# Stick-breaking attention: key evacuation, split weights and sample sums reordered, half of the sample key products moved to GpSimd

## The chip, the cores and the metric

One core of one Trainium2 chip runs the whole program: two layers of a small decoder for a prompt of 512 tokens and 8 sample tokens. The metric is the device time of one execution in microseconds (us). Only the attention of layer 0 is touched.

## The reference, cut to what matters

Each of the 8 samples has one query and 512 past positions in 4 cached pages of 128. Per head, the score is the dot product of the query with every cached key; a sigmoid of it, times the product of the complements of all later positions, weighs the cached values. The prompt's 512 tokens do the same among themselves.

```python
z = jnp.einsum('bqhd,bkhd->bhqk', q, k).astype(jnp.float32) * scale + bias
log_not = jnp.where(mask, jax.nn.log_sigmoid(-z), 0.0)
after = lax.cumsum(log_not, axis=3, reverse=True) - log_not
a = jnp.where(mask, jnp.exp(jax.nn.log_sigmoid(z) + after), 0.0)
return jnp.einsum('bhqk,bkhd->bqhd', a.astype(v.dtype), v)
```

## The kernel before

The channels are split into 8 head pairs (`hp`, 0 to 7). Attention is a loop over them written out by hand, one list of steps per engine, joined by semaphores. Each list is executed strictly in its order, so a step that waits holds everything behind it on its engine.

In pass `hp` the prompt's attention for head pair `hp` runs: scores (TensorE, `scores`), two sigmoids for each of five score units (ScalarE, `sigmoids`), a running product and the weights (VectorE, `later_product`, a scan, and `weights`), transposes of the weights (TensorE and ScalarE, `turned`), outputs (`output_a`, `output_b`). Between them TensorE computes the k and v of head pair `hp + 1` in eight pieces, `chunk(hp, 0..7)`: pieces 0 to 3 make k, pieces 4 to 7 make v. Weights are kept as a high and a low part: ScalarE's `split_hi` (L227) and VectorE's `split_lo` (L231, `w_lo<-w_raw,w_hi`). VectorE's `next_v(hp)` makes the low part that `chunk(hp, 4)` waits for, `next_k(hp)` that of the next pass. `k_evac` (L293, `s_up<-ps,rms`) takes k out of PSUM; ScalarE squares it (`k_squares`, L1074), TensorE sums over heads (`k_sums`, L800), ScalarE takes the root (`k_factor`, L1081 and L1083), VectorE's `ready` (L1266) normalizes, and TensorE transposes it in `k_turned` (L825).

The same loop carries sample `hp` and, ahead of it, the scores of sample `hp + 1`. SyncE spreads the sample's query over 128 partitions into `q_bc` (it lies in the tile `p_tok`), and loads four key pages into `kc`, 128x1024 each. `page_scores(b, g)` multiplies page g by the query in place (L1330) and reduces over each head (L1335). In pass 0 VectorE does all four pages of sample 0 as well as those of sample 1. `page_sums` (L1347 to L1353) prepares later-position sums, TensorE's `sample_sums` (L956 and L957) adds them up, `page_weights` (L1358) subtracts them; the next `k_turned` waits for that, since they share a PSUM bank. `sample_exp` (ScalarE, L1180) makes the weights of the sample, `sample_values` and `sample_output` (TensorE) apply them. Keys of the next sample are loaded page by page by `next_keys`, each page after the reduction of the old one. GpSimd does nothing in this loop except one memset at its start (L1438).

The order of VectorE's list behind the last weights of a pass is:

```python
weights(hp, 4); next_v(hp)
# pass 0 only: page_scores(0, 0..3), page_bias(0)
k_evac(hp + 1); next_k(hp)
page_scores(hp + 1, 0); ready(hp + 1)
page_scores(hp + 1, 1); page_sums(hp)
page_scores(hp + 1, 2); sample_lo(hp - 2)
page_weights(hp); pair_lo(hp)
page_scores(hp + 1, 3); page_bias(hp + 1)
```

TensorE's list in the same place is `turned` 0, 1, 2, `k_sums(hp + 1)`, `turned` 3, `chunk` 4, `turned` 4, `chunk` 5, `sample_output(hp - 2)`, `output_a`, `chunk` 6, `output_b`, `sample_sums(hp)`, `k_turned(hp + 1)`, `chunk` 7.

Of the kernel before, what the change touches and what calls it, by code (L numbers as in the profile page):

```python
# [22 lines left out]
NS = 8  # L23
# [25 lines left out]
def build(nc, io):  # L49
# [4 lines left out]
    with ctx:  # L54
# [3 lines left out]
        def sem(name):  # L58
            return ctx.enter_context(nc.semaphore(name))
# [604 lines left out]
        k_out = sem("k_out")  # L664
        v_out = sem("v_out")
        kq_ok = sem("kq_ok")
        z_mm = sem("z_mm")
        sm_ok = sem("sm_ok")
        sg_ok = sem("sg_ok")
# [31 lines left out]
            return ps[:, 2 + r // 2, r % 2, :]  # L701

        cs_ps = ps[:, 0, 1, HALF:HALF + PG * NH]

        def os_at(b):
            return bank(min(b + 2, NP - 1), OS)[:, 0:KD]
# [10 lines left out]
        def attn_sp(sp):  # L717
            n0 = M["slab"]

            def kv(hp, c):  # L720
                load_slab(sp, n0 + NP + 2 * hp + c, c, qkv_src(1 + c, hp), KD)

            def page_of(cache, dst, done, b, g):

                page = sp.value_load(pages[0:1, b * PG + g:b * PG + g + 1], min_val=0, max_val=cache.shape[1] - 1)
                rows = cache[0].rearrange("n p h d -> n p (h d)")[ds(page, 1), :, :]
                sp.dma_start(dst[:, g, :], rows.rearrange("a p f -> p (a f)")).then_inc(done[g], 16)

            def k_page(b, g):
                page_of(io["cache_k"], kc, k_cache_in, b, g)  # L730

            def v_page(b, g):
                page_of(io["cache_v"], vc, v_cache_in, b, g)

            def q_spread(b):
                sp.dma_start(q_bc, q_rows[b:b + 1, :].broadcast_to([P, D])).then_inc(q_bc_in, 16)

            for m in range(NP):
                load_slab(sp, n0 + m, m % 2, qkv_src(0, m), KD)
            sp.wait_ge(first_in[3], 16)  # L740
            sp.wait_ge(slab_used, n0)
            for g in range(PG):
                k_page(0, g)
            for g in range(PG):
                v_page(0, g)
            for hp in range(2):
                for c in range(2):
                    kv(hp, c)
            for c in range(2):
                sp.wait_ge(qt_ok, c + 1)  # L750
                sp.dma_start(q_rows[:, c * TP:(c + 1) * TP], q_row[c]).then_inc(q_rows_in, 16)
            sp.wait_ge(q_rows_in, 32)
            q_spread(0)

            def next_keys(b):
                sp.wait_ge(kq_ok, PG * b)
                q_spread(b)
                for g in range(PG):
                    sp.wait_ge(zs_ok, 5 * (b - 1) + g + 1)
                    k_page(b, g)  # L760

            for hp in range(NP):
                if hp + 2 < NP:
                    kv(hp + 2, 0)
                elif hp + 2 == NP:
                    load_slab(sp, n0 + 3 * NP, 0, slab_src(io["attn_w_o"][0], 0), KD)
                if hp >= 2:
                    sp.wait_ge(sv_mm, hp - 1)
                    for g in range(PG):
                        v_page(hp - 1, g)  # L770
                if hp + 2 < NP:
                    kv(hp + 2, 1)
                elif hp + 2 == NP:
                    load_slab(sp, n0 + 3 * NP + 1, 1, slab_src(io["attn_w_o"][0], 1), KD)
                if hp == 0:
                    next_keys(1)
                if hp + 2 < NS:
                    next_keys(hp + 2)
                elif hp + 2 == NS:
                    for g in range(PG):  # L780
                        sp.wait_ge(zs_ok, 5 * (NS - 1) + g + 1)
                        page_of(io["cache_v"], kc, k_cache_in, NS - 1, g)

        def attn_pe(pe):
# [50 lines left out]
            def k_sums(hp):  # L835
                head_sums(NP + hp, 0, 0)
# [156 lines left out]
            for hp in range(NP - 1):  # L993
                scores(hp, (0, 1))
                scores(hp, (2, 3))
                v_turned(hp)
                scores_last(hp)
                chunk(hp, 0)
                chunk(hp, 1)
                if hp >= 2:  # L1000
                    pe.wait_ge(vt_ok, 2 * hp + 2)
                    sample_values(hp - 2)
                chunk(hp, 2)
                chunk(hp, 3)
                turned(hp, 0)
                turned(hp, 1)
                turned(hp, 2)
                k_sums(hp + 1)
                turned(hp, 3)
                chunk(hp, 4)  # L1010
                turned(hp, 4)
                chunk(hp, 5)
                if hp >= 2:
                    sample_output(hp - 2)
                output_a(hp)
                chunk(hp, 6)
                output_b(hp)
                sample_sums(hp)
                k_turned(hp + 1)
                chunk(hp, 7)  # L1020

# [238 lines left out]
        def attn_dve(dve, prev_evac, prev_lo):  # L1260
# [63 lines left out]
                                  ALU.mult).then_inc(a_ok, 1)  # L1324

            def page_scores(b, g):
                if g == 0:
                    dve.wait_ge(q_bc_in, 16 * b + 16)
                dve.wait_ge(k_cache_in[g], 16 * b + 16)
                dve.tensor_tensor(kc[:, g, :], kc[:, g, :], q_bc, ALU.mult).then_inc(kq_ok, 1)  # L1330
                dve.wait_ge(kq_ok, PG * b + g + 1)
                if b >= 2:
                    dve.wait_ge(aw_ok, b - 1)
                    dve.wait_ge(zw_ok, 4 * b - 4)
                dve.tensor_reduce(zs[:, b % 2, g, :], kc[:, g, :].rearrange("p (h d) -> p h d", d=HD),  # L1335
                                  AX.X, ALU.add).then_inc(zs_ok, 1)
# [43 lines left out]
            def next_v(hp):  # L1380
                split_lo(dve, n0 + NP + 2 * hp + 3, 1)
# [10 lines left out]
            for hp in range(NP):  # L1392
                more = hp + 1 < NP
                v_evac(hp)
                later_product(hp, 0)
                later_product(hp, 1)
                weights(hp, 0)
                later_product(hp, 2)
                weights(hp, 1)
                later_product(hp, 3)  # L1400
                weights(hp, 2)
                later_product(hp, 4)
                weights(hp, 3)
                if hp >= 2:
                    sample_own(hp - 2)
                weights(hp, 4)
                next_v(hp)
                if hp == 0:
                    for g in range(PG):
                        page_scores(0, g)  # L1410
                    page_bias(0)
                if more:
                    k_evac(hp + 1)
                    next_k(hp)
                    page_scores(hp + 1, 0)
                    ready(hp + 1)
                    page_scores(hp + 1, 1)
                    page_sums(hp)
                    page_scores(hp + 1, 2)
                    if hp >= 2:  # L1420
                        sample_lo(hp - 2)
                    page_weights(hp)
                    pair_lo(hp)
                    page_scores(hp + 1, 3)
                    page_bias(hp + 1)
                else:
                    page_sums(hp)
                    page_weights(hp)
                    sample_own(hp - 1)
                    sample_lo(hp - 2)  # L1430
                    sample_lo(hp - 1)
                    pair_lo(hp)
                    sample_own(hp)
                    sample_lo(hp)

        def attn_pool(pool):
            pool.wait_ge(slab_used, M["slab"])
            pool.memset(aw[:, :, :, :], 0.0).then_inc(aw_set, 1)  # L1438


        C = at["mix", 1]
# [561 lines left out]
        def _(sp):  # L2003
            load_sp(sp)
            for layer in LAYERS:
                up_sp(sp, at["up1", layer], layer, io["ffn1_wg"], io["ffn1_wu"])
                to_x_sp(sp, at["down1", layer], 2, io["ffn1_wd"][layer])
                if layer == 0:
                    attn_sp(sp)
                    to_x_sp(sp, at["mixout", 0], 1, io["attn_w_o"][0], loaded=2)  # L2010
                    sp.wait_ge(kq_ok, PG * NS)
                    sp.wait_ge(k_out, 32 * NP)
                    sp.wait_ge(v_out, 32 * NP)
                    load_p(sp, 0)
                else:
                    conv_sp(sp)
                    conv_out_sp(sp)
                    conv_tail_sp(sp)
                up_sp(sp, at["up2", layer], layer, io["ffn2_wg"], io["ffn2_wu"])
                to_x_sp(sp, at["down2", layer], 2, io["ffn2_wd"][layer])  # L2020
                ple_sp(sp, at["ple", layer], layer)
# [104 lines left out]
```

## Time and profile before

| | |
|---|---|
| time, median of 3 runs | 2323.81 us (2322.67 to 2325.43) |
| the profiled execution's own time | 2320.65 us |
| its span | 2318.8 us |
| TensorE matmul busy | 2217.2 us (96%) |
| VectorE, ScalarE, GpSimd busy | 1083.5, 751.8, 120.2 us |
| mean granted TensorE clock | 0.982 |

The span is the stretch between the first and the last instruction. A row of a window of time gives its start and end, its length, the busy time (and number of instructions) of TensorE's matmuls, TensorE's weight loads, VectorE, ScalarE and GpSimd, then TensorE's granted clock, the share of time that the DMA engines were busy, and GB/s. A granted clock of 1.0 is full speed (2.4 GHz), 0.5 is half (1.2 GHz). The attention passes lie between 477 and 740 us of the span. Each instruction is shown with its line in the source; the line can be that of a helper, and then the names of its output and inputs tell which step it is. Pass `hp` is counted here from `k_turned(hp)` to `k_turned(hp + 1)`.

### The profile page before, as it was taken

How to read it: one execution, taken by the hardware profiler on the slowest of the kernel's cores; microseconds unless marked ns; L12 is line 12 of the kernel's file. 1: busy time of each engine (PE TensorE's matmuls, PEld its weight loads, DVE VectorE, ACT ScalarE, POOL GpSimd, SP SyncE). 2: the span in 40 equal slices, each digit the busy share in tenths (PEclk: the TensorE clock that was granted, in tenths of full speed). 3: DMA queues.
4: the chain of work that ended last, by engine and by line, in shares of the span. 5: the costliest groups of instructions: out<-in, count | busy, mean ns of one | idle time of the engine just before them, and what ended most of it. 6: DMA issues, size and time to landing. Idle time of an engine off the chain costs nothing.

```text
span 2318.8 us, 43547 instructions
## 1 busy us (share of the span) xinstructions
PE 2217.2 (96%) x18009; PEld 2116.0 (91%) x18009; DVE 1083.5 (47%) x1273; ACT 751.8 (32%) x1011; POOL 120.2 (5%) x97
## 2 busy tenths in 40 slices
PE   7999999978898999999999999999798899999998
PEld 7999999957777999999999999999665899999998
DVE  5444433368785444443355444433633544443344
ACT  4222222445663422222234222222111532222223
POOL 2000001000000100000110000001300100000100
PEclk9999999989998999999999999999899999999999
DMA  3333333435663333333232333333442233333322
GB/s 113 91 90 90 104 87 89 146 107 168 218 219 118 99 92 91 91 100 91 80 91 82 90 90 90 100 99 90 108 124 79 62 89 92 92 92 96 98 70 83
DMA packets 380347, 237.98 MB, mean 103 GB/s; under 512 B 10090, under 2 KB 363850, under 8 KB 380264
## 3 DMA queue, kind: packets, MB, share of 16 engines
q1 hardware_dynamic: 371560, 232.56, 33.9%
q10 hardware_dynamic: 8704, 4.26, 0.6%
q8 instruction: 59, 0.97, 0.2%
q14 instruction: 24, 0.20, 0.0%
HBM read 220.36 MB, written 7.53 MB: 98 GB/s over the span
## 4 chain that ended last, share of the span: by engine, by line
PE 84%; DVE 6%; ACT 3%; issue 3%; SPq 3%; DMA 1%; ACTq 0%; DVEq 0%
PE ps L242 79%; SPq L1482 2%; PE ps L1533 2%; DVE w_lo L231 1%; DVE kc L1330 1%; DVE sg_m L1316 1%; PE ps L1868 1%; DVE sg_p L1323 1%; DVE zs L1335 0%; ACT sg_m L1155 0%; ACT w_hi L227 0%; SPq L1494 0%; DVE h_lo L259 0%; ACT sg_p L1159 0%; ACT a_t L1173 0%
## 5 line engine op out<-in xcount | busy, mean ns | idle before, releaser
L242 PE MATMUL ps<-h_hi,w_hi 128*128 128x260 f32 x3712 | 758.9, 286 | 4.5 <-DVE h_lo L259 4.5
L242 PE MATMUL ps<-h_hi,w_lo 128*128 128x260 f32 x3712 | 750.5, 284 | 0.0
L242 PE MATMUL ps<-h_lo,w_hi 128*128 128x260 f32 x3712 | 749.2, 283 | 0.0
L227 ACT ACTIVATE w_hi<-w_raw 128x1024 fp32r<-128x1024 f32 (+1 forms) x314 | 353.9, 1127 | 1141.7 <-PE ps L242 1099.5
L242 PEld LDWEIGHTS ps<-h_hi,w_hi 128*128 128x128 f32 x3712 | 576.9, 190 | 12.7 <-issue 8.1
L242 PEld LDWEIGHTS ps<-h_hi,w_lo 128*128 128x128 f32 x3712 | 574.9, 189 | 0.0
L242 PEld LDWEIGHTS ps<-h_lo,w_hi 128*128 128x128 f32 x3712 | 574.1, 189 | 0.0
L231 DVE TENSOR_TENSOR w_lo<-w_raw,w_hi 128x1024 fp32r<-128x1024 f32 (+1 forms) x316 | 420.0, 1329 | 278.7 <-ACT w_hi L227 278.3
L242 PE MATMUL ps<-a_hi,w_hi 128*128 128x260 f32 x1408 | 283.7, 283 | 0.0
L242 PE MATMUL ps<-a_hi,w_lo 128*128 128x260 f32 x1408 | 283.1, 282 | 0.0
L242 PE MATMUL ps<-a_lo,w_hi 128*128 128x260 f32 x1408 | 282.5, 282 | 0.0
L293 DVE TENSOR_TENSOR s_up<-ps,rms 128x520 f32<-128x520 f32 x108 | 75.5, 699 | 338.3 <-PE ps L242 332.1
L242 PEld LDWEIGHTS ps<-a_lo,w_hi 128*128 128x128 f32 x1408 | 217.3, 188 | 0.0
L242 PEld LDWEIGHTS ps<-a_hi,w_hi 128*128 128x128 f32 x1408 | 216.7, 188 | 0.0
L242 PEld LDWEIGHTS ps<-a_hi,w_lo 128*128 128x128 f32 x1408 | 216.6, 188 | 0.0
L293 DVE TENSOR_TENSOR s_gate<-ps,rms 128x520 f32<-128x520 f32 x116 | 81.1, 699 | 188.6 <-PE ps L242 149.1
L299 DVE SCALAR_TENSOR_TENSOR x<-ps,x 128x520 f32 (+1 forms) x42 | 29.4, 700 | 199.0 <-PE ps L242 199.0
L317 ACT ACTIVATE a_hi<-s_prod 128x520 f32 (+1 forms) x88 | 56.2, 639 | 176.3 <-DVE s_prod L324 176.3
L272 POOL TENSOR_TENSOR sumsq<-sumsq,square 128x520 f32<-128x520 f32 x56 | 87.4, 1561 | 480.4 <-ACT square L255 450.1
L326 DVE TENSOR_TENSOR a_lo<-s_prod,a_hi 128x520 f32 (+1 forms) x88 | 61.6, 701 | 80.7 <-ACT a_hi L317 80.7
L269 POOL COPY sumsq<-square 128x520 f32<-128x520 f32 x8 | 6.7, 840 | 1630.0 <-ACT square L255 1606.3
L259 DVE SCALAR_TENSOR_TENSOR h_lo<-x,gains,h_hi 128x520 fp32r<-128x520 f32 (+1 forms) x64 | 80.5, 1266 | 3.4 <-ACT h_hi L253 2.0
(214 smaller groups left out, 1554.7 us busy)
## 6 DMA issues: line engine op xcount, KB each, us to landing
w_raw<-in_ffn_wg SPq DMA_DIRECT2D x88, 512.0 KB, 3.8
w_raw<-in_ffn_wu SPq DMA_DIRECT2D x88, 512.0 KB, 3.8
w_raw<-in_ffn_wd SPq DMA_DIRECT2D x64, 704.0 KB, 4.4
kc<-in_cache_k SPq DMA_DIRECT2D x32, 512.0 KB, 5.3
vc<-in_cache_v SPq DMA_DIRECT2D x28, 512.0 KB, 5.2
w_raw<-in_attn_w_qkv SPq DMA_DIRECT2D x24, 512.0 KB, 5.3
g<-g_pad SPq DMA_DIRECT2D x128, 67.0 KB, 2.1
w_raw<-in_ple_w_gate SPq DMA_DIRECT2D x16, 512.0 KB, 3.7
```

The costliest lines, as they stand in the source:

```text
L227: act.activation(w_hi[:, j, 0:cols], w_raw[:, j, 0:cols], ACT.Copy).then_inc(slab_hi, 1)
L231: dve.tensor_tensor(w_lo[:, j, 0:cols], w_raw[:, j, 0:cols], w_hi[:, j, 0:cols].bitcast(F32), ALU.subtract).then_inc(slab_lo, 1)
L242: ins = pe.matmul(out[:, b_, :], a[:, j, w], b[:, k0 + k, b_ * HALF:(b_ + 1) * HALF], start=(first and k == kts[0] and n == 0), stop=(last ...
L259: dve.scalar_tensor_tensor(h_lo[:, ds(m, 1), :].rearrange("p a t -> p (a t)"), x[:, ds(m, 1), :].rearrange("p a t -> p (a t)"), gain_col(l ...
L272: pool.tensor_tensor(sumsq[:, :], sumsq[:, :], square[:, m2, :], ALU.add).then_inc(acc_ok, 1)
L293: dve.tensor_tensor(halves(out), slot(s), halves(rms[:, :]), ALU.mult).then_inc(evac, 1)
L299: dve.scalar_tensor_tensor(xm, slot(s), factor, xm, ALU.mult, ALU.add).then_inc(evac, 1)
L317: act.activation(a_hi[:, ds(f, 1), :].rearrange("p a t -> p (a t)"), s_prod[:, :], ACT.Copy).then_inc(a_hi_ok, 1)
L326: dve.tensor_tensor(a_lo[:, ds(f, 1), :].rearrange("p a t -> p (a t)"), s_prod[:, :], a_hi[:, ds(f, 1), :].rearrange("p a t -> p (a t)").b ...
L1316: ins = dve.tensor_tensor_scan(m, m, zero[:, :].broadcast_to([P, (i + 1) * P]), 1.0, ALU.mult, ALU.max)
L1482: sp.dma_start(g4[j * Q:(j + 1) * Q, k % 2, g, :], g_pad[g * Q:(g + 1) * Q, k % 2, j:j + GW]).then_inc(g4_in[k % 2], 16)
L1533: ins = pe.matmul(ps[g * Q:(g + 1) * Q, 3, k % 2, :], diag4[:, k, g, i, :], g4[:, k % 2, g, 4 * i:4 * i + TP], start=i == 0, stop=i == GRO ...
```

## The change

Three things are changed.

- VectorE's list: `k_evac(hp + 1)` stands right behind the last weights, ahead of `next_v(hp)`; the page scores of sample 0 come behind `next_k(0)`; `page_sums(hp)` comes ahead of `page_scores(hp + 1, 1)`, and `page_weights(hp)` right behind it, ahead of `page_scores(hp + 1, 2)`.
- TensorE's list: `k_sums(hp + 1)` stands behind `chunk(hp, 4)`, and `sample_sums(hp)` behind `output_a(hp)`, ahead of `chunk(hp, 6)` and `output_b(hp)`.
- GpSimd does the products of all four pages of sample 0 and of pages 2 and 3 of every other sample. It starts those of sample b when the query has landed, VectorE's last weights of pass b - 1 are done (`a_ok`), and the page has landed. VectorE keeps all the reductions.

```diff
+        def on_gpsimd(b, g):
+            return b == 0 or g >= 2
+        def kp_count(b, g):
+            return g + 1 if b == 0 else PG + 2 * (b - 1) + max(g - 1, 0)
...
             def next_keys(b):
-                sp.wait_ge(kq_ok, PG * b)
+                sp.wait_ge(kp_ok, kp_count(b - 1, PG - 1))
+                if b > 1:
+                    sp.wait_ge(kq_ok, PG * b - kp_count(b - 1, PG - 1))
...
                 turned(hp, 2)
-                k_sums(hp + 1)
                 turned(hp, 3)
                 chunk(hp, 4)
+                k_sums(hp + 1)
...
                 output_a(hp)
+                sample_sums(hp)
                 chunk(hp, 6)
                 output_b(hp)
-                sample_sums(hp)
...
             def page_scores(b, g):
-                if g == 0:
+                if on_gpsimd(b, g):
+                    dve.wait_ge(kp_ok, kp_count(b, g))
+                else:
                     dve.wait_ge(q_bc_in, 16 * b + 16)
-                dve.wait_ge(k_cache_in[g], 16 * b + 16)
-                dve.tensor_tensor(kc[:, g, :], kc[:, g, :], q_bc, ALU.mult).then_inc(kq_ok, 1)
-                dve.wait_ge(kq_ok, PG * b + g + 1)
+                    dve.wait_ge(k_cache_in[g], 16 * b + 16)
+                    dve.tensor_tensor(kc[:, g, :], kc[:, g, :], q_bc, ALU.mult).then_inc(kq_ok, 1)
+                    dve.wait_ge(kq_ok, PG * b + g + 1 - kp_count(b, g))
...
-                next_v(hp)
-                if hp == 0:
-                    for g in range(PG):
-                        page_scores(0, g)
-                    page_bias(0)
                 if more:
                     k_evac(hp + 1)
+                    next_v(hp)
                     next_k(hp)
+                    if hp == 0:
+                        for g in range(PG):
+                            page_scores(0, g)
+                        page_bias(0)
                     page_scores(hp + 1, 0)
                     ready(hp + 1)
+                    page_sums(hp)
                     page_scores(hp + 1, 1)
-                    page_sums(hp)
-                    page_scores(hp + 1, 2)
+                    page_weights(hp)
                     if hp >= 2:
                         sample_lo(hp - 2)
-                    page_weights(hp)
+                    page_scores(hp + 1, 2)
                     pair_lo(hp)
                     page_scores(hp + 1, 3)
                     page_bias(hp + 1)
...
         def attn_pool(pool):
+            for b in range(NS):
+                if not on_gpsimd(b, PG - 1):
+                    continue
+                pool.wait_ge(q_bc_in, 16 * b + 16)
+                if b:
+                    pool.wait_ge(a_ok, UNITS * b)
+                for g in range(PG):
+                    if on_gpsimd(b, g):
+                        pool.wait_ge(k_cache_in[g], 16 * b + 16)
+                        pool.tensor_tensor(kc[:, g, :], kc[:, g, :], q_bc, ALU.mult).then_inc(kp_ok, 1)
```

## Rows read from the trace of the kernel before

**Rows 1.** The page: busy time of the engines, and the key pages' DMA issues.

```profile
PE 2217.2 (96%) x18009; PEld 2116.0 (91%) x18009; DVE 1083.5 (47%) x1273; ACT 751.8 (32%) x1011; POOL 120.2 (5%) x97
...
kc<-in_cache_k SPq DMA_DIRECT2D x32, 512.0 KB, 5.3
```

**Rows 2.** Windows: end of pass 0 (from 486), passes 2 and 5.

```profile
486.00:515.74 29.74, 16.64 (x123) 14.74 (x121) 26.05 (x34) 12.30 (x22) 0.00 (x0) 0.77 0.32 107
...
545.62:576.80 31.18, 27.08 (x218) 21.65 (x218) 25.35 (x37) 18.20 (x34) 0.00 (x0) 1.00 0.62 203
...
639.16:670.33 31.17, 28.62 (x218) 23.18 (x219) 25.35 (x37) 18.21 (x34) 0.00 (x0) 0.95 0.62 204
```

**Rows 3.** Waits on TensorE over the attention passes: total, times, longest.

```profile
PE ps L825 <- DVE zs L1358: 6.5, 7, 1.9
```

**Rows 4.** Timeline of VectorE in pass 5: start, us, instruction, idle before.

```profile
653.97 0.68 DVE L1323 TENSOR_TENSOR sg_p<-sg_p,sg_m 128x511 f32<-128x511 f32 x1
...
655.70 0.69 DVE L293 TENSOR_TENSOR s_up<-ps,rms 128x520 f32<-128x520 f32 x1
...
670.06 0.21 DVE L1358 TENSOR_TENSOR zs<-zs,ps 128x64 f32<-128x64 f32 x1
```

**Rows 5.** Timeline of TensorE in pass 5.

```profile
653.77 1.47 PE L900 MATMUL ps<-ident,sg_p 128*128 128x128 f32 x12
657.11 1.21 PE L800 MATMUL ps<-square,head_ones 128*128 128x260 f32 x4 [1.88 <-ACT square L1074]
...
658.11 1.06 PE L900 MATMUL ps<-ident,sg_p 128*128 128x128 f32 x4
658.83 0.78 PE L242 MATMUL ps<-h_hi,w_hi 128*128 128x260 f32 x2
...
667.08 0.51 PE L242 MATMUL ps<-h_hi,w_hi 128*128 128x260 f32 x2
...
670.33 0.66 PE L825 MATMUL ps<-ident,k_f 128*128 128x128 f32 x4 [0.38 <-DVE zs L1358]
```

**Rows 6.** Timeline of GpSimd outside the attention.

```profile
1197.43 1.32 POOL L272 TENSOR_TENSOR sumsq<-sumsq,square 128x520 f32<-128x520 f32 x1 [3.62 <-ACT square L1924]
...
1634.82 5.43 POOL L1817 TENSOR_TENSOR st<-st,taps 128x1920 f32<-128x1920 f32 x1 [16.61 <-DVE st L1725]
...
1646.54 2.14 POOL L1824 TENSOR_TENSOR diag<-ident,tap 128x896 f32<-128x896 f32 x1
```

**Rows 7.** Timeline of VectorE at the same times.

```profile
1635.26 6.08 DVE L231 TENSOR_TENSOR w_lo<-w_raw,w_hi 128x1024 fp32r<-128x1024 f32 x1
...
1647.04 0.69 DVE L293 TENSOR_TENSOR s_gate<-ps,rms 128x520 f32<-128x520 f32 x1
1647.65 2.10 DVE L231 TENSOR_TENSOR w_lo<-w_raw,w_hi 128x1024 fp32r<-128x1024 f32 x1
```

**Rows 8.** Groups of instructions on GpSimd: a small product.

```profile
L535 POOL TENSOR_TENSOR head_at<-head_at,ident 128x16 f32<-128x16 f32 x2 | 0.4, 220 | 0.2
```

**Rows 9.** Timeline of ScalarE: the square that releases GpSimd's product at 1197.43.

```profile
1196.72 0.64 ACT L1924 ACTIVATE square<-x 128x520 f32<-128x520 f32 x1 [2.11 <-DVE x L1988]
```

**Rows 10.** Timeline of TensorE in pass 0.

```profile
503.19 2.10 PE L800 MATMUL ps<-square,head_ones 128*128 128x260 f32 x4 [12.34 <-ACT square L1074]
```

**Rows 11.** Timeline of VectorE in pass 0.

```profile
484.92 1.27 DVE L1316 TENSOR_TENSOR_SCAN sg_m<-sg_m,zero 128x384 f32<-128x384 f32 x2 [0.99 <-ACT sg_m L1155]
...
490.83 1.22 DVE L231 TENSOR_TENSOR w_lo<-w_raw,w_hi 128x1024 fp32r<-128x1024 f32 x1
...
501.77 0.69 DVE L293 TENSOR_TENSOR s_up<-ps,rms 128x520 f32<-128x520 f32 x1
```

**Rows 12.** Timeline of SyncE's DMA issues in pass 0.

```profile
479.90 0.36 SPq L736 DMA_DIRECT2D p_tok<-q_rows  x1
...
501.66 3.67 SPq L727 DMA_DIRECT2D kc<-in_cache_k  x4
```

**Rows 13.** The query tile: time from issue to landing.

```profile
DMA to landing us min/median/max: 3.9/4.4/5.8
```

More of the change, by code:

```diff
@@ L666, in build @@
         kq_ok = sem("kq_ok")
+        kp_ok = sem("kp_ok")
         z_mm = sem("z_mm")
@@ L1426, in attn_dve @@
                 else:
+                    next_v(hp)
                     page_sums(hp)
@@ L2010, in _ @@
                     to_x_sp(sp, at["mixout", 0], 1, io["attn_w_o"][0], loaded=2)
-                    sp.wait_ge(kq_ok, PG * NS)
+                    sp.wait_ge(kp_ok, kp_count(NS - 1, PG - 1))
+                    sp.wait_ge(kq_ok, PG * NS - kp_count(NS - 1, PG - 1))
                     sp.wait_ge(k_out, 32 * NP)
```

## The prediction

> **What bounds the kernel now.** The page comes first: TensorE is busy 96% of the span, so only the places where it stands still can give anything [rows 1]. Windows over the attention passes show where: the end of pass 0 has 16.64 us of matmul in 29.74 us; passes 2 and 5 last 31.2 us each with 27.1 and 28.6 us of it [rows 2]. They are equally long although TensorE's granted clock is 1.00 in one and 0.95 in the other. So TensorE isn't the bound there. The waits say what is: `k_turned` waits for `page_weights` on VectorE, seven times, up to 1.9 us [rows 3]. A pass is a ring: VectorE's last weights, its list of key and sample work, `page_weights`, `k_turned`, the next scores. Inside the ring TensorE has one long hole: the three transposes end at 655.24, and `k_sums` begins at 657.11 after 1.88 us idle, because VectorE splits weights before it takes k out [rows 4, 5]. In pass 0 that hole is 12.34 us [rows 10], since all of sample 0's pages stand before the evacuation: last weights until 490.9, k evacuated at 501.77 [rows 11].
>
> **The price of GpSimd.** No product of 128x1024 on GpSimd is in the trace. Two plain ones are: 16 elements in 0.22 us [rows 8], 520 in 1.32 us with no VectorE work on two tiles beside it [rows 6]. The line through them is 0.19 us + 2.2 ns for each, 2.4 us for 1024. Bounds: the 896-element products, which took 2.14 us beside VectorE, in proportion 2.4 but with a wait in it, so 1.9 below; 1920 elements in 5.43 us, in proportion 2.9 above [rows 6].
>
> More important is what happens to VectorE meanwhile. `w_lo` from two SBUF tiles takes 1.22 us [rows 11], but 6.08 us when it starts at 1635.26, with GpSimd at a product since 1634.82: GpSimd ends at 1640.25 and `w_lo` 1.09 us later [rows 6, 7]. Another `w_lo` starts at 1647.65, GpSimd's product ends at 1648.68, `w_lo` at 1649.75 [rows 6, 7]. So it is held to the end of the GpSimd product and then needs 1.1 us. `s_gate<-ps,rms`, one operand in PSUM, takes its usual 0.69 us in the middle of the same product [rows 7]. After each held instruction VectorE got its turn, although more GpSimd products were queued: the engines alternate.
>
> The Trainium skill, "SBUF — State Buffer", section "Who interferes with whom", states the same as a lock: a VectorE instruction with two SBUF inputs and a GpSimd instruction that reads SBUF exclude each other for the whole instruction. The trace agrees (6.08 us). Its "GPSIMD Engine Reference", "Engine selection", would leave such products on VectorE; its 4497 ns for 2048 elements would make an estimated 2.25 us here, 0.15 us less than mine in each use below.
>
> **Passes 1 to 6, step by step, in the times of pass 5.** Nothing is altered until the last weights end, 653.97 + 0.68 = 654.65 [rows 4]. Then:
> - GpSimd starts page 2 at about 654.7 and ends at 657.1.
> - `k_evac` has a PSUM operand, isn't held, and ends at 655.3 instead of 656.4. That part works.
> - `next_v` would start at 655.2, is held to 657.1, ends at 658.2 (before: about 655.8, where the evacuation starts).
> - `chunk 4` now stands ahead of `k_sums`, so TensorE resumes at 658.25, not 657.11: +1.14 us. It stands still 2.5 us instead of 1.9, `turned` 3 being done before.
> - `turned` 3 out of the way: 658.83 - 658.11 = 0.7 us at the lower clock, half of it at full speed [rows 5].
> - From the restart to `k_turned` TensorE has the same work as before in another order (670.33 - 657.11 = 13.2 us, of which 0.38 is waiting) [rows 5].
> - GpSimd takes page 3 at 658.2 and holds `next_k` to 660.6; it ends at 661.7. VectorE then has product, reduction, `ready`, `page_sums`, product, reduction: 1.2 + 1.2 + 0.7 + 0.6 + 1.2 + 1.2, so `page_weights` at about 668 to 669 against 670.06 before. Two products less (2.4 us) are paid for by two holds, but `page_weights` is no longer last. TensorE is.
>
> In a pass at full speed TensorE waited 1.9 us at `k_turned` [rows 3]; now it doesn't: +1.14 - 0.35 - 1.9 = -1.1 us. In a pass with a clock dip the dip lay in that wait; now it is on the path. The dip cost 0.05 x 31.17 = 1.5 us in pass 5 [rows 2], so about -1.1 + 1.5 = +0.4, and up to +1.1 if it lasts longer after the longer hole. Before, the shorter hole left one of the two passes shown at full speed; with 2.5 us of standing still I count a dip of +0.7 in seven of ten: 0.7 x 0.7 - 0.3 x 1.1 = +0.15 us, for six passes +0.9, between -6.6 (no dip) and +6.6 (+1.1 in each). GpSimd at 1.9 or 2.9 us moves TensorE's restart by 0.5 us, 3 us over six passes, either way.
>
> **Pass 0.** The query is issued at 479.90 and lands at 484.3 [rows 12, 13]. GpSimd then does four products, 9.6 us, in turn with VectorE's scans and weights, all on two SBUF inputs, which have 5.9 us left (484.92 to 490.9) [rows 11]. Last weights: 484.3 + 9.6 + 5.9 = 499.8. Evacuation ends at 500.4 (before 502.5), `next_v` at 501.5, `next_k` at 503.7, sample 0's first reduction at 504.9. Only then may the first key page of sample 1 be loaded: issue about 505.8 against 501.66 before [rows 12], landing 5.3 us later [rows 1] at 511.1, the others 1.2 us apart. VectorE: product 512.3, reduction 513.5, `ready` 514.1. Page 2 has landed at 513.5, so GpSimd takes its turn to 516.5, before the rest of `page_sums` page 3 to 519.0, and the sums end at 519.3. `sample_sums`, which TensorE now waits for ahead of `chunk` 6 and `output_b`, comes then; the three take 670.33 - 0.38 - 667.08 = 2.9 us [rows 5], twice that at half clock after so long a pause: `k_turned(1)` at 522 to 525, before 515.74. If page 2 lands 0.6 us later, `page_sums` goes first and `k_turned(1)` comes at 518 to 520. Bounds +2 and +9 us. The two orders are apart by less than the spread of a landing (3.9 to 5.8 us [rows 13]); I take +6. If GpSimd doesn't hold the scans (no row shows one beside it), all comes up to 4 us earlier: +2.
>
> SyncE's altered waits are hidden: later key pages are asked for earlier than before and used 10 us after landing. The tail, pass 7, is unaltered.
>
> **Sum.** +6 + 0.9 = +6.9 us on the profiled execution's 2320.65: 2327.6. The median of the runs, 2323.81, lies 3.2 us above it: 2331.
>
> **The rivals.**
> - *Forecast: held VectorE eats the gain, pass 0 loses.* 51%: 2331, own range 2324 to 2338; 43 of the 51 points lie above +0.2%.
> - *`page_sums` goes first in pass 0, or scans aren't held.* +2 to +4 in all: 2327. 27%, counted as no change.
> - *VectorE gets `next_v` in before page 2.* It decides if GpSimd starts more than 0.45 us after the last weights. Then `chunk` 4 starts 1.8 us earlier in six passes: +6.9 - 10.8 = -3.9 or, with fewer dips, -7: 2317. Against it: GpSimd began 0.07 us after its releaser (1197.43 against 1197.36, the end of ScalarE's square [rows 6, 9]). 8%.
> - *No holding between these products.* `next_v` ends at 656.4, the hole is 0.8 us, without a dip: some -3 us in six passes, and in pass 0 -8: -26, 2298. The 6.08 us speaks against it. 7%.
> - *GpSimd takes both pages before VectorE's turn.* 2.4 us more in six passes: +6.9 + 14.4 = +21, 2345. The alternation seen in the trace speaks against it. 7%.
>
> **Range and chances.** 2319 to 2338 holds the forecast, its milder form and part of the third. 0.2% (4.6 us) is about what a measurement of this kernel can tell from no change. Faster 0.17 (both fast rivals, 2 of the forecast's), within 0.2% 0.33, slower 0.50.
>
> **What would show it.** In the changed trace: GpSimd's products 2.4 us each, more if they wait; `next_v` stretched from 1.2 to about 3 us in passes 1 to 6, `next_k` likewise; `chunk` 4 starting 3.6 us after the last weights; TensorE idle 2.5 us there; no wait at `k_turned`. In pass 0 scans and weights held in turn, `k_sums` at about 503 to 505, and a long wait at `sample_sums`. I am wrong if `next_v` keeps its 1.2 us, if clock dips vanish, or if pass 0 is shorter than before.

## The result

| | before | changed |
|---|---|---|
| median of 15 executions each | 2322.35 us | 2317.88 us |
| ratio, 95% interval | | 0.998 [0.9973, 0.9988] |
| profiled execution: span, mean granted clock | 2318.8 us, 0.982 | 2314.3 us, 0.983 |

The change makes the kernel 0.2% faster, 4.5 us by the medians. The forecast was 2331 us, slower, with 2319 to 2338 as its range: wrong in sign.

Windows of the changed kernel from one `k_turned` to the next, passes 0 to 6, then the two stretches behind them (start and end, length, then TensorE, its weight loads, VectorE, ScalarE, GpSimd, granted clock, DMA share, GB/s):

```profile
476.80:517.00 40.20, 27.18 (x174) 21.72 (x175) 32.48 (x33) 18.59 (x34) 15.46 (x6) 0.80 0.38 119
517.00:546.56 29.56, 24.98 (x188) 20.99 (x186) 24.71 (x31) 18.11 (x33) 6.48 (x3) 0.93 0.46 147
546.56:577.82 31.26, 28.34 (x221) 22.98 (x219) 27.43 (x35) 18.19 (x34) 5.66 (x2) 0.95 0.64 213
577.82:607.54 29.72, 26.83 (x220) 21.55 (x218) 26.90 (x35) 18.20 (x34) 5.68 (x2) 1.00 0.65 212
607.54:638.87 31.33, 28.44 (x221) 22.95 (x219) 26.94 (x35) 18.20 (x34) 5.67 (x2) 0.95 0.63 201
638.87:670.02 31.15, 28.26 (x220) 22.90 (x219) 26.91 (x35) 18.20 (x34) 5.67 (x2) 0.95 0.62 203
670.02:699.76 29.74, 26.84 (x220) 21.55 (x219) 26.95 (x35) 18.20 (x34) 5.69 (x2) 1.00 0.67 221
699.76:737.27 37.51, 31.44 (x239) 22.68 (x238) 18.55 (x33) 15.25 (x32) 0.00 (x0) 0.91 0.46 141
737.27:784.20 46.93, 46.93 (x391) 46.93 (x392) 20.94 (x25) 18.53 (x25) 13.02 (x8) 1.00 0.34 101
```

In the profile of the kernel before, all passes from 2 to 6 took 31.2 us, at a granted clock of 1.00 as at 0.95 [rows 2]. Now the length follows the clock: 29.7 us at 1.00, 31.2 to 31.3 us at 0.95. TensorE's own work and its hole behind the last weights set the length, no longer `page_weights`, as forecast. In this pair of profiles pass 0 costs 1.5 us more (38.7 before), passes 1 to 6 together take 3.0 us less (185.8 before, 182.8 now), and 2.8 us come from what lies behind the last `k_turned` (1617.3 before, 1614.5 now), where the steps of pass 7 and all behind them are unaltered; 0.3 us lie ahead of pass 0. The granted clock of the first stretches there differs. The kernel before:

```profile
701.50:740.00 38.50, 32.48 (x237) 22.62 (x238) 19.28 (x33) 14.66 (x31) 0.00 (x0) 0.87 0.40 127
740.00:788.42 48.42, 48.42 (x391) 48.42 (x392) 20.94 (x25) 18.53 (x25) 13.04 (x8) 0.96 0.33 98
```

VectorE in pass 5 of the changed kernel:

```profile
653.67 0.68 DVE L1332 TENSOR_TENSOR sg_p<-sg_p,sg_m 128x511 f32<-128x511 f32 x1
654.27 0.69 DVE L293 TENSOR_TENSOR s_up<-ps,rms 128x520 f32<-128x520 f32 x1
654.88 6.37 DVE L231 TENSOR_TENSOR w_lo<-w_raw,w_hi 128x1024 fp32r<-128x1024 f32 x2
661.17 1.21 DVE L1341 TENSOR_TENSOR kc<-kc,p_tok 128x1024 f32<-128x1024 f32 x1
...
668.95 0.21 DVE L1369 TENSOR_TENSOR zs<-zs,ps 128x64 f32<-128x64 f32 x1
```

GpSimd at the same time, a row for each of the two products:

```profile
654.49 2.36 POOL L1460 TENSOR_TENSOR kc<-kc,p_tok 128x1024 f32<-128x1024 f32 x1 [25.65 <-DVE sg_p L1332]
...
656.82 3.35 POOL L1460 TENSOR_TENSOR kc<-kc,p_tok 128x1024 f32<-128x1024 f32 x1
```

TensorE at the same time:

```profile
657.99 0.80 PE L242 MATMUL ps<-h_hi,w_hi 128*128 128x260 f32 x2 [2.60 <-DVE w_lo L231]
...
660.75 1.24 PE L809 MATMUL ps<-square,head_ones 128*128 128x260 f32 x4
...
670.02 0.66 PE L834 MATMUL ps<-ident,k_f 128*128 128x128 f32 x4
```

GpSimd starts 0.14 us after the last weights and needs 2.36 us for page 2. `next_v` and `next_k`, the two `w_lo`, take 6.37 us together instead of 2 x 1.2. Between the two GpSimd products `next_v` has its turn, and the second product shows 3.35 us, 1.0 us of it waiting. `chunk` 4 starts 3.64 us after the last weights, behind a hole of 2.60 us, where before it was 1.88 [rows 5]; and `k_turned` no longer waits [rows 3, 5]. The forecast has each of these times within 0.15 us. Together they explain why the change brings so little. They do not explain the sign of the forecast; that takes pass 0 and the clock, below.

### The profile page after: what moved, and what is told of

Same layout as the page of the kernel before. It is cut to its first block, busy times and chain, and to the rows that moved or that the text cites. A ratio compares the mean times of both kernels' runs of the same rounds, so it can differ in the third digit from the quotient of the medians.

```text
span 2314.3 us, 43568 instructions
## 1 busy us (share of the span) xinstructions
PE 2215.1 (96%) x18009; PEld 2117.0 (91%) x18009; DVE 1094.2 (47%) x1255; ACT 751.9 (32%) x1011; POOL 170.3 (7%) x115
## 4 chain that ended last, share of the span: by engine, by line
PE 87%; DVE 5%; SPq 3%; ACT 2%; issue 2%; DMA 1%; ACTq 0%; DVEq 0%
PE ps L242 81%; SPq L1505 2%; PE ps L1556 2%; DVE w_lo L231 1%; DVE sg_m L1325 1%; PE ps L1891 1%; PE ps L957 1%; PE ps L809 1%; DVE sg_p L1332 0%; PE ps L924 0%; ACT sg_m L1164 0%; SPq L1517 0%; ACT sg_p L1168 0%; DMA g<-g_pad 0%; DMA xs_tok<-in_x_sample 0%
## 5 line engine op out<-in xcount | busy, mean ns | idle before, releaser
L231 DVE TENSOR_TENSOR w_lo<-w_raw,w_hi 128x1024 fp32r<-128x1024 f32 (+1 forms) x316 | 443.5, 1405 | 263.1 <-ACT w_hi L227 262.7
```

Source lines behind the costliest of these rows:

```text
L231: dve.tensor_tensor(w_lo[:, j, 0:cols], w_raw[:, j, 0:cols], w_hi[:, j, 0:cols].bitcast(F32), ALU.subtract).then_inc(slab_lo, 1)
```

## The experiments

Ratios are against the kernel before, measured on the same chip, with 95% intervals.

**The new order alone.** All products stay on VectorE.

```diff
         def on_gpsimd(b, g):
-            return b == 0 or g >= 2
+            return False
```

> The new order on TensorE and VectorE, with all key products left on VectorE. If the new order brings the gain and GpSimd's products only hold VectorE back: next_v keeps 1.2 us, chunk 4 starts 1.8 us after the last weights instead of 3.6, TensorE has no dip there, VectorE's longer list (2.4 us more per pass) becomes the bound at about 29.6 us per pass; six passes give -9, pass 0 +2, together about -7 us against before (2315). If moving products to GpSimd is what brings the gain: 0 or slower than before.

Measured: 2308.14 us, ratio 0.9943 [0.993, 0.9957], 13 us under the 2321.56 of before. The windows of passes 2 and 5:

```profile
543.75:573.28 29.53, 27.04 (x221) 21.60 (x219) 25.30 (x37) 18.23 (x34) 0.00 (x0) 1.00 0.62 214
...
631.60:660.61 29.01, 27.04 (x220) 21.61 (x219) 25.22 (x37) 18.23 (x34) 0.00 (x0) 1.00 0.65 219
```

TensorE waits 1.1 to 1.6 us ahead of `chunk` 4 in passes 2 to 6, without a dip, and 0.8 to 0.9 us for VectorE's `s_act` in the next pass. So the reordering is the gain, and moving the products costs about 9 us of it. My expectation (-7) was too small: passes 2 to 6 are 29.2 us on average, not 29.6, and pass 1 is 26.9 us against 29.9 before, at a granted clock of 1.00 against 0.89. The +2 us of pass 0 came as expected (40.8 against 38.7).

**GpSimd alone, in the old order.** The kernel before with the change's counts, its `page_scores` and GpSimd's products; the lists of `k_evac` and the values stay as before. The core of the diff:

```diff
+        def on_gpsimd(b, g):
+            return b == 0 or g >= 2
...
-                if g == 0:
+                if on_gpsimd(b, g):
+                    dve.wait_ge(kp_ok, kp_count(b, g))
+                else:
...
+            for b in range(NS):
+                pool.wait_ge(q_bc_in, 16 * b + 16)
+                if b:
+                    pool.wait_ge(a_ok, UNITS * b)
```

> The old order with GpSimd's products. next_v stands right behind the last weights and starts before GpSimd does, so it isn't held; next_k is held by page 3 (about 1.9 us), two products are saved (2.4 us), pass 0 loses 3 us because the scans are held before the evacuation: -1 us per pass, together about -3 us. If the order is what counts and GpSimd brings nothing: 0 to +5 us.

Measured: 2319.58 us, ratio 0.9988 [0.9978, 0.9998]: 2 to 3 us less. The sum is as expected, its parts are not, so that is partly luck: in the profiles pass 0 costs 4.4 us more (43.1 against 38.7; 3 expected), and passes 1 to 6 give 1.9 us (183.9 against 185.8; 6 expected). VectorE in a pass of it:

```profile
596.20 1.22 DVE L231 TENSOR_TENSOR w_lo<-w_raw,w_hi 128x1024 fp32r<-128x1024 f32 x1
597.34 0.69 DVE L293 TENSOR_TENSOR s_up<-ps,rms 128x520 f32<-128x520 f32 x1
600.16 2.90 DVE L231 TENSOR_TENSOR w_lo<-w_raw,w_hi 128x1024 fp32r<-128x1024 f32 x1 [2.13 <-ACT w_hi L227]
```

GpSimd's products are released by the same weights, but here `next_v` begins first (596.20, GpSimd at 596.42) and isn't held. It is the change's own order, `k_evac` with its PSUM operand in between, that lets GpSimd in ahead of `next_v`.

**GpSimd's start behind `next_v`.**

```diff
-                    pool.wait_ge(a_ok, UNITS * b)
+                    pool.wait_ge(slab_lo, M["slab"] + NP + 2 * (b - 1) + 4)
```

> As the changed kernel, but GpSimd's products of samples 1 to 7 wait for next_v instead of the last weights. If the hold of next_v costs the passes: chunk 4 starts 1.8 us after the last weights, no dip, passes of 28.4 to 29 us, 11 to 14 us less than before. If the hold lies beside other work that is late anyway: same as the changed kernel, -4.5 us.

Measured: 2310.22 us, ratio 0.9954 [0.9941, 0.9968]. `next_v` is free, `next_k` and the product of page 0 are held instead:

```profile
619.47 1.21 DVE L231 TENSOR_TENSOR w_lo<-w_raw,w_hi 128x1024 fp32r<-128x1024 f32 x1
621.68 2.59 DVE L231 TENSOR_TENSOR w_lo<-w_raw,w_hi 128x1024 fp32r<-128x1024 f32 x1 [1.00 <-ACT w_hi L227]
624.20 3.39 DVE L1341 TENSOR_TENSOR kc<-kc,p_tok 128x1024 f32<-128x1024 f32 x1
```

What is late next is `page_sums`, for which TensorE's `sample_sums` waits, and a pass takes 29.35 us at full clock:

```profile
620.73 0.51 PE L242 MATMUL ps<-h_hi,w_hi 128*128 128x260 f32 x2 [0.72 <-DVE w_lo L231]
630.12 0.43 PE L965 MATMUL ps<-w_raw,from_here 128*128 128x64 f32 x2 [1.37 <-DVE runs L1364]
```

My 28.4 to 29 left that wait out, but the direction stands: with `next_v` free passes 1 to 6 take 175.9 us, 6.8 less than in the changed kernel's first profile. That is net of what the hold of `next_k` and of page 0's product costs instead.

**GpSimd's products cut to 16 columns** in pages 2 and 3 of samples 1 to 7, so that almost all of the work is gone and the order stays. The kernel leaves out the other 1008 columns, so the scores of those pages are not the reference's.

```diff
-                        pool.tensor_tensor(kc[:, g, :], kc[:, g, :], q_bc, ALU.mult).then_inc(kp_ok, 1)
+                        cols = D if b == 0 else 16
+                        pool.tensor_tensor(kc[:, g, 0:cols], kc[:, g, 0:cols], q_bc[:, 0:cols], ALU.mult).then_inc(kp_ok, 1)
```

> As the changed kernel, but GpSimd multiplies only 16 of the 1024 columns of pages 2 and 3 of samples 1 to 7 (the scores of those pages are not the reference's). It shows what all holding costs together: passes of about 28.2 us, 16 us less than before. If the holding costs nothing: same as the changed kernel.

Measured: 2301.34 us, ratio 0.9916 [0.9903, 0.993], passes of 27.9 us. The long products in passes 1 to 6, VectorE held by them, cost the changed kernel 2317.88 - 2301.34 = 16.5 us (medians of different sittings; 182.8 - 166.4 = 16.4 us between the two profiles, over passes 1 to 6).

**GpSimd beside VectorE's reductions.** Pages 2 and 3 of every sample, each started by VectorE's product of page 0 and page 1.

```diff
-            return b == 0 or g >= 2
+            return g >= 2
...
-                if b:
-                    pool.wait_ge(a_ok, UNITS * b)
...
                         pool.wait_ge(k_cache_in[g], 16 * b + 16)
+                        pool.wait_ge(kq_ok, 2 * b + g - 1)
```

> The changed kernel with GpSimd's product of page 2 (of every sample) started when VectorE's product of page 0 is done, and page 3 when that of page 1 is done, so that they run beside VectorE's reductions and its wait for the sample's weights, which take one input. If it is only the place of GpSimd's products that costs: nothing held but short pieces, passes of 27.9 to 28.5 us as with the cut-down products, 16 to 20 us less than before. If any product on GpSimd costs VectorE its length wherever it lies: passes of 29.4 us or more, no better than the new order alone (-13 us).

Measured: 2301.17 us, ratio 0.9917 [0.9904, 0.993]. VectorE in one pass of it:

```profile
616.59 1.22 DVE L1340 TENSOR_TENSOR kc<-kc,p_tok 128x1024 f32<-128x1024 f32 x1
619.79 1.22 DVE L1345 TENSOR_REDUCE zs<-kc 128x16 f32<-128x1024 f32 x1 [1.98 <-issue]
620.93 0.75 DVE L1274 SCALAR_TENSOR_TENSOR k_f<-s_up,qk_gain,s_prod 128x520 f32<-128x520 f32 x1
...
623.40 1.22 DVE L1345 TENSOR_REDUCE zs<-kc 128x16 f32<-128x1024 f32 x1
624.54 0.21 DVE L1368 TENSOR_TENSOR zs<-zs,ps 128x64 f32<-128x64 f32 x1
624.66 0.17 DVE L1384 TENSOR_TENSOR o_lo<-ps,o_hi 128x8 fp32r<-128x8 f32 x1
624.74 1.21 DVE L1345 TENSOR_REDUCE zs<-kc 128x16 f32<-128x1024 f32 x1
```

GpSimd in the same pass of the same kernel:

```profile
617.98 2.38 POOL L1458 TENSOR_TENSOR kc<-kc,p_tok 128x1024 f32<-128x1024 f32 x1 [20.00 <-DVE kc L1340]
623.51 2.38 POOL L1458 TENSOR_TENSOR kc<-kc,p_tok 128x1024 f32<-128x1024 f32 x1 [3.15 <-DVE kc L1340]
```

The same two products, 2.38 us each, lie beside VectorE's own wait, the reductions (1.2 us as ever) and operations with a PSUM operand (0.2 us as ever). No VectorE instruction of this pass is held, and passes 2 to 6 take 27.9 us, as with the products cut down. In passes 1 to 6 the place of the products is all that costs.

**Sample 0's products on VectorE.** The changed kernel otherwise.

```diff
-            return b == 0 or g >= 2
+            return b > 0 and g >= 2
```

> The changed kernel with all of sample 0's products on VectorE behind next_k(0); passes 1 to 7 as changed. GpSimd no longer holds the scans of pass 0, so the last weights of pass 0 end at 490.6 instead of 498.6, but VectorE has 4.9 us more before the first reduction of sample 1, and the query of sample 1 is only spread after the fourth product. If pass 0 is bound by the landing of sample 1's keys behind sample 0's work: pass 0 within 1.5 us of 40.2, the time within 1.5 us of the changed kernel. If the holding of the scans is what costs pass 0: 5 to 8 us less.

Measured: 2323.69 us, ratio 1.0013 [1.0004, 1.0022]: 5.8 us more than the changed kernel by the medians of different sittings, outside both expectations. Passes 1 to 6 are 182.7 us, as in the changed kernel; pass 0 is 44.56 us. There VectorE was held in the middle of `page_sums`:

```profile
510.70 0.75 DVE L1275 SCALAR_TENSOR_TENSOR k_f<-s_up,qk_gain,s_prod 128x520 f32<-128x520 f32 x1
511.37 2.36 DVE L1358 SCALAR_TENSOR_TENSOR w_raw<-zs,w_raw 128x64 f32<-128x64 f32 x1
513.77 2.21 DVE L1361 TENSOR_TENSOR runs<-w_raw 128x16 f32<-128x16 f32 x1
```

VectorE at the same place in the changed kernel:

```profile
508.44 1.23 DVE L1341 TENSOR_TENSOR kc<-kc,p_tok 128x1024 f32<-128x1024 f32 x1 [1.02 <-DMA kc<-in_cache_k]
...
511.50 0.22 DVE L1358 SCALAR_TENSOR_TENSOR w_raw<-zs,w_raw 128x64 f32<-128x64 f32 x1
511.75 0.18 DVE L1361 TENSOR_TENSOR runs<-w_raw 128x16 f32<-128x16 f32 x1
```

GpSimd there, in the changed kernel:

```profile
512.12 5.71 POOL L1460 TENSOR_TENSOR kc<-kc,p_tok 128x1024 f32<-128x1024 f32 x2 [17.51 <-DMA kc<-in_cache_k]
```

In the changed kernel page 2 of sample 1 landed at 512.1, just as `page_sums` was through. Here GpSimd started at 511.20, 0.2 us ahead of `page_sums`, which began as early as in the changed kernel (511.37 against 511.50) and was through 4 us later. This is the order that the forecast's +6 to +9 us were made of; pass 0 is 44.6 - 40.2 = 4.4 us longer than with the other, and 5.9 us longer than before.

One pass of this kernel shows a rival of the forecast too. In pass 3 the last weights end at 596.06, and GpSimd's row begins 0.50 us behind them, in the other passes 0.13 to 0.14 us; this once `next_v` has its turn first. The rows are GpSimd, VectorE and TensorE:

```profile
596.56 3.49 POOL L1460 TENSOR_TENSOR kc<-kc,p_tok 128x1024 f32<-128x1024 f32 x1 [24.39 <-DVE sg_p L1332]
596.59 1.21 DVE L231 TENSOR_TENSOR w_lo<-w_raw,w_hi 128x1024 fp32r<-128x1024 f32 x1
597.86 0.51 PE L242 MATMUL ps<-h_hi,w_hi 128*128 128x260 f32 x2 [0.75 <-DVE w_lo L231]
```

`chunk` 4 starts 1.80 us after the last weights instead of 3.6, and the pass takes 29.1 us, 0.6 less than one at full clock with `next_v` held. Why GpSimd was late there, no run shows.

**Pass 0: `page_sums` ahead of sample 1's keys**, on top of GpSimd beside the reductions.

```diff
+                    if hp == 0:
+                        ready(1)
+                        page_sums(0)
+                        page_weights(0)
                     page_scores(hp + 1, 0)
-                    ready(hp + 1)
-                    page_sums(hp)
+                    if hp:
+                        ready(hp + 1)
+                        page_sums(hp)
                     page_scores(hp + 1, 1)
-                    page_weights(hp)
+                    if hp:
+                        page_weights(hp)
```

> As the kernel with GpSimd beside the reductions, and in pass 0 ready(1), page_sums(0) and page_weights(0) come ahead of page_scores(1, 0). If pass 0 waits for sample 1's keys on VectorE ahead of page_sums(0): sample_sums comes 5 us or so earlier and the time falls by 3 to 6 us more. If the scores of sample 1 only move into pass 1 and hold its scans: no change.

Measured: 2297.4 us, ratio 0.9892 [0.9876, 0.9908], the lowest median of all, though the interval overlaps that of the kernel it builds on. Pass 0 falls from 39.3 to 33.0 us; pass 1, which now gets sample 1's scores, grows from 26.7 to 30.3. Net that is -2.7 us for the two passes, -0.9 for the profiles' whole spans and -3.8 by the medians (of 4 and 5 executions).

**Further profiles of the two kernels.**

> The changed kernel once more, for a second profile. If the part behind the attention passes (the last k_turned to the end: 1617.3 us before, 1614.5 us in the changed kernel's first profile) is the same work at a clock that falls out differently from one execution to the next, it comes out anywhere in 1614 to 1620 us, as the other profiles do (1616.6, 1617.0, 1619.6, 1617.4). If the change shortened it, it is 1614.5 again. Passes 2 to 6 again last 29.7 us without and 31.2 us with a clock dip, in other numbers.

> The changed kernel, unaltered, for a third profile: passes 1 to 6 together 182.6 to 182.8 us and the part behind them 1614.5 to 1615.1 us as in the first two, if the clock falls out alike each time; otherwise passes 2 to 6 with another number of dips (1.5 us each), and the part behind them up to 5 us longer.

> The kernel before, unaltered, for a second profile. If the clock falls out alike in every execution of a kernel: passes of 31.2 us, pass 0 38.7 us, the part behind the attention passes 1617.3 us again, with mean clocks of 0.87 and 0.96 in its first 38 and next 52 us. If it falls out at random: that part anywhere in 1614 to 1620 us.

| | pass 0 | passes 1 to 6 | behind the last `k_turned` | span |
|---|---|---|---|---|
| before | 38.7 | 185.8 | 1617.3 | 2318.8 |
| before, second | 38.1 | 189.0 | 1621.0 | 2324.7 |
| changed | 40.2 | 182.8 | 1614.5 | 2314.3 |
| changed, second | 40.0 | 182.6 | 1615.1 | 2313.9 |
| changed, third | 39.6 | 183.2 | 1617.8 | 2316.4 |

The second profile of the kernel before shows what the first had hidden. The windows of its passes 2 and 4:

```profile
544.56:577.33 32.77, 30.22 (x219) 24.72 (x219) 25.45 (x37) 18.23 (x34) 0.00 (x0) 0.90 0.59 193
...
608.50:639.69 31.19, 27.08 (x219) 21.64 (x219) 25.37 (x37) 18.20 (x34) 0.00 (x0) 1.00 0.58 203
```

Passes 2 and 5 take 32.8 us there, at a mean clock of 0.90. Rows of passes 2 and 4 show why: first `k_turned(2)`, then a window behind `k_turned` in each pass (with its granted clock), then the last weights of each.

```profile
544.56 1.11 PE L825 MATMUL ps<-ident,k_f 128*128 128x128 f32 x4 [1.87 <-DVE zs L1358]
...
545.00:547.00 2.00, 2.00 (x12) 1.92 (x11) 1.97 (x3) 0.74 (x2) 0.00 (x0) 0.50 0.00 0
609.00:611.00 2.00, 2.00 (x17) 1.80 (x16) 1.97 (x3) 0.74 (x2) 0.00 (x0) 1.00 0.00 0
...
560.96 0.68 DVE L1323 TENSOR_TENSOR sg_p<-sg_p,sg_m 128x511 f32<-128x511 f32 x1
...
623.32 0.68 DVE L1323 TENSOR_TENSOR sg_p<-sg_p,sg_m 128x511 f32<-128x511 f32 x1
```

Pass 2 has two dips, and the first lies right behind `k_turned`, where TensorE computes the scores that VectorE needs for its weights. The last weights come 16.4 us after `k_turned` there, in pass 4 14.8 us. Behind them both passes take 16.37 us, with a dip (pass 2) and without (pass 4). So a dip behind the last weights is hidden in the wait at `k_turned`, and one ahead of them isn't: what counts is where it lies. Both early dips followed a wait of 1.9 us at `k_turned` (1.87 and 1.95); after the same waits of 1.95 and 1.94 in the first profile none came. The changed kernel no longer waits there, and its passes 2 to 6 are nowhere longer than 31.3 us in three profiles.

The part behind the passes is the same work in all kernels; it took 1614.5 to 1621.0 us in the twelve profiles. Neither of my two readings of it holds strictly: it is not alike from one execution of a kernel to the next (1617.3 and 1621.0; 1614.5 and 1617.8), and the changed kernel's three lie low. Whether the change shifts the clock there on average stays open.

## Why the prediction was wrong

**What bounds the kernel, and the price of GpSimd.** Right. The product was priced at 2.4 us and takes 2.36; VectorE is held as the rows of before showed; the engines alternate; an operation with a PSUM operand and a reduction are not held. The Trainium skill's rule in "SBUF — State Buffer", "Who interferes with whom", that a VectorE instruction with two SBUF inputs and a GpSimd instruction that reads SBUF shut each other out, agrees with every case above (6.37 us for two `w_lo`, 2.36 for 64 columns, reductions at their usual 1.2). The scans of pass 0, which no row of before showed beside a product, are held too; VectorE in the changed kernel:

```profile
484.63 5.09 DVE L1325 TENSOR_TENSOR_SCAN sg_m<-sg_m,zero 128x384 f32<-128x384 f32 x2 [0.98 <-ACT sg_m L1164]
489.64 2.76 DVE L1332 TENSOR_TENSOR sg_p<-sg_p,sg_m 128x511 f32<-128x511 f32 x1
```

against 1.27 us for two [rows 11].

**Pass 0, the failing term.** Forecast +6 us, measured +1.5 (40.2, 40.0, 39.6 against 38.7, 38.1). Up to the key loads the forecast was 1.1 us late: loads issued at 504.7, not 505.8. The landing was mis-sized: page 0 landed at 508.4, 3.7 us after its issue, not the 5.3 of the median over all key pages [rows 1]. Before, the query was sent 1.3 us ahead of the keys (at 500.37, and the keys at 501.66 [rows 12]), now 3.8 us ahead. Page 2 landed 7.4 us after the issue, near the 7.7 of the forecast, so it is page 0's early landing that put `page_sums` ahead. With sample 0 on VectorE the query went out 1.3 us ahead again, page 0 landed 4.5 us after its issue and page 2 again 7.4, and GpSimd came first. I worked out both orders of page 2 and `page_sums`, saw that 0.6 us decide between them, and put a number between the two. What ran is `page_sums` first, and it was cheaper than its own forecast (+1.5, not +2 to +4). The experiment with sample 0 on VectorE shows the other order with its 44.6 us, +5.9 where +6 was forecast, so the mechanism was right, and the choice of the order and the landing were not.

**Passes 1 to 6, the second failing term.** Forecast +0.9, measured -3.0 in the first pair of profiles and -2.6 to -6.4 over all pairs. Three parts: without a dip the pass is 1.45 us shorter, not 1.1; with a dip it is as long as before (31.2), not 0.7 longer, since the dip cost 1.5 us and no more after the longer hole; and dips came in three of five passes, not seven of ten. The fourth lies in the kernel before: I read 31.2 us as the length of its passes whatever the clock, from one execution, although the forecast itself has the scores in the ring. A dip that falls into them isn't hidden; the other profile has two such passes of 32.8.

**Sum.** With the terms as the first profiles show them, 1.5 - 3.0 = -1.5 us, no measurable change. Most of the other 3 us of the measured 4.5 lie behind the passes in these two profiles (2.8 us), at a granted clock that differs between them; over many executions longer passes of the old kernel may count too. That it is all clock was not shown, and five profiles cannot divide it. From the forecast's 2331 to the measured 2317.88 there are 13.1 us: 4.5 from pass 0, 3.9 from passes 1 to 6, 3.0 from parts for which nothing was forecast, and 1.4 because I added 3.2 us from the profiled execution to the median, where the changed kernel has 1.8 (2317.88 against 2316.07); the rest is rounding.

**The rivals.** `page_sums` first in pass 0 was listed with 27% and is what ran, at 2327; its passes were forecast too long. `next_v` ahead of page 2 didn't happen in the changed kernel's profiles but does in the old order, and in one pass with sample 0 on VectorE: `chunk` 4 came 1.8 us earlier, as priced, but the pass was only 0.6 us shorter. No holding, and both pages before VectorE's turn, are excluded by the rows above.

## What to carry to other kernels

Before moving elementwise work to GpSimd, list what VectorE does in those microseconds: beside reductions, operations with a PSUM operand and VectorE's own waits two products of 2.4 us cost nothing here, beside operations on two SBUF tiles the same two products cost 2.7 us per pass and took most of what the reordering had earned. Test the reordering and the move apart: here one was worth -13 us, the other gave 9 of them back, and with only its start moved it brought a further 6 to 7. When two events 0.6 us apart decide a term, forecast the two cases, not their mean; and take a pass length that "doesn't depend on the clock" from more than one execution.

## What was not expected of the hardware

- The first key page of sample 1 (512 KB) landed 3.5 to 3.8 us after its issue in the five profiles where the query, of the same size, had been issued 3.8 us ahead of it, and 4.2 to 5.4 us after it in the six where that was 1.3 us (503.82 to 508.87, for one, in the kernel with the new order alone).
- A VectorE operation of 64 columns on two SBUF tiles (0.22 us) took 2.36 us beside a GpSimd product, and one of 16 columns (0.18 us) 2.21 us: the hold is as long as GpSimd's instruction, however small VectorE's is.
- The same hole of 1.87 us on TensorE was followed by a stretch of low clock (0.95 over the pass) in some passes and by none in others, and two executions of one kernel differed in which: in the kernel before, pass 3 was at 1.00 in one and at 0.95 in the other. Holes of 2.6 us in the changed kernel were followed by none in two of five passes. The shorter holes of passes 2 to 6 were never followed by one (new order alone: 1.1 to 1.6 us; beside the reductions: 0.7 to 0.8).
